# Four more groups of the convolution input product by Strassen's scheme in the projection phase, and half the filler work in the second attention

## The reference

```
h = rms_norm(x, norm1_g)
proj = einsum('bsd,de->bse', h, w_in)          # w_in 1024 x 6144
q, k, v, bg, cg, xc = split(proj)              # six times 1024 features
y_attn = chunked_relpos_attention(q, k, v, ...)  # 16 heads of 64, own chunk of 64 and the 8 before
y_conv = bg * conv_width3(cg * xc)
gates  = sigmoid(einsum(h, w_gate) + b_gate)   # w_gate 1024 x 2048
merged = g_attn * (y_attn @ w_attn_proj) + g_conv * (y_conv @ w_conv_proj)
x = x + merged @ w_out
x = x + square(relu(rms_norm(x, norm2_g) @ w_up)) @ w_down
```

## Time and profile before

| | us |
|---|---|
| median of 3 runs | 2182.41 |
| lowest, highest | 2175.3, 2184.18 |
| the profiled execution's own time | 2176.62 |
| its span, first to last instruction | 2174.9 |

### The profile page before, as it was taken

The page is one execution under the profiler, slowest core; times in us unless marked ns, Lnnn a source line. Parts: engine busy times, 40 slices in busy tenths (PEclk is TensorE's granted clock), DMA queues, the critical chain, the costliest instruction groups (busy, mean ns, idle before and its releaser), DMA issues.

```text
span 2174.9 us, 29102 instructions
## 1 busy us (share of the span) xinstructions
PE 2147.4 (99%) x10450; PEld 1788.1 (82%) x10450; DVE 1480.9 (68%) x2585; ACT 950.3 (44%) x1696; POOL 999.6 (46%) x701
## 2 busy tenths in 40 slices
PE   8999999999999999999999999999999999999999
PEld 8888888888777888888888888788878888788887
DVE  7776775255875666666666658642786777898886
ACT  5555425343232555555555531211555455533332
POOL 3232465454545331313132246547465655666564
PEclk9999999999999999999999999999999999999999
DMA  6320123332135332324243256315144445826433
GB/s 230 104 76 21 45 94 148 126 117 101 55 116 156 103 94 88 99 77 112 67 109 82 75 185 248 115 49 184 59 132 157 167 150 180 328 93 227 151 121 116
DMA packets 198606, 269.34 MB, mean 124 GB/s; under 512 B 58136, under 2 KB 116280, under 8 KB 198368
## 3 DMA queue, kind: packets, MB, share of 16 engines
q1 hardware_dynamic: 124880, 201.38, 27.1%
q10 hardware_dynamic: 73616, 66.49, 10.0%
HBM read 191.23 MB, written 85.00 MB: 127 GB/s over the span
## 4 chain that ended last, share of the span: by engine, by line
PE 82%; DVE 8%; ACT 3%; issue 3%; POOL 2%; DMA 1%; ACTq 1%; POOLq 0%; DVEq 0%; SPq 0%
PE ps L204 71%; PE ps L2333 3%; PE ps L2308 2%; PE ps L2320 2%; PE ps L776 1%; PE ps L751 1%; PE ps L762 1%; DVE k_lo L2553 1%; POOL w_lo L3191 1%; DVE a_lo L446 1%; POOL w_lo L1887 1%; DVE qkv_head_stat L2145 1%; PE ps L2345 1%; DVE pt_lo L2601 0%; ACT pt_hi L2487 0%
## 5 line engine op out<-in xcount | busy, mean ns | idle before, releaser
L204 PE MATMUL ps<-a_hi,w_hi 128*128 128x512 f32 x1376 | 537.1, 407 | 6.0 <-POOL w_lo L1887 3.7
L159 POOL TENSOR_TENSOR w_hi<-w_raw,zero 128x512 fp32r<-128x512 f32 x172 | 201.2, 1200 | 735.9 <-PE ps L204 612.4
L204 PE MATMUL ps<-a_hi,w_lo 128*128 128x512 f32 x1376 | 516.9, 393 | 0.0
L204 PE MATMUL ps<-a_lo,w_hi 128*128 128x512 f32 x1376 | 514.0, 391 | 0.0
L204 PE MATMUL ps<-w_hi,a_hi 128*128 128x512 f32 (+1 forms) x960 | 369.4, 385 | 7.3 <-POOL w_lo L1887 3.5
L204 PE MATMUL ps<-w_hi,a_lo 128*128 128x512 f32 (+1 forms) x960 | 367.6, 383 | 0.0
L204 PE MATMUL ps<-w_lo,a_hi 128*128 128x512 f32 (+1 forms) x960 | 367.5, 383 | 0.0
L204 PEld LDWEIGHTS ps<-a_hi,w_lo 128*128 128x128 f32 x1376 | 258.4, 188 | 57.6
L204 PEld LDWEIGHTS ps<-a_hi,w_hi 128*128 128x128 f32 x1376 | 258.9, 188 | 50.0 <-POOL w_lo L1887 4.5
L204 PEld LDWEIGHTS ps<-a_lo,w_hi 128*128 128x128 f32 x1376 | 259.8, 189 | 40.8
L164 POOL TENSOR_TENSOR w_lo<-w_raw,w_hi 128x512 fp32r<-128x512 f32 x172 | 243.9, 1449 | 3.4
(11 more groups left out here) (307 smaller groups left out, 3938.1 us busy)
## 6 DMA issues: line engine op xcount, KB each, us to landing
mlp_part<-u_parts SPq DMA_DIRECT2D x26, 1024.0 KB, 7.9
w_raw<-in_w_in_dram SPq DMA_DIRECT2D x24, 1024.0 KB, 5.3
feat_fm<-stage ACTq DMA_DIRECT2D x68, 256.0 KB, 2.1
u_parts<-mlp_acc SPq DMA_DIRECT2D x28, 512.0 KB, 2.8
u_parts<-res SPq DMA_DIRECT2D x28, 512.0 KB, 2.8
conv_in<-feat_fm ACTq DMA_DIRECT2D x24, 512.0 KB, 5.1
res<-in_x_dram SPq DMA_DIRECT2D x16, 512.0 KB, 6.5
w_raw<-in_w_out_dram SPq DMA_DIRECT2D x8, 1024.0 KB, 5.0
```

What stands on the lines that cost most here:

```text
L159: hi = nc.gpsimd.tensor_tensor(w_hi[slot][:, k:k + 2, :], w_raw[:, k:k + 2, :], zero[:, 0:1].unsqueeze(2).to_broadcast([P, 2, CW]), ALU.add)
L204: last = nc.tensor.matmul(out_of(o), lhs, rhs(o), start=first and n == 0, stop=final and n == 2)
```

## The change

1. `BCX_GROUPS` goes from 1 to 5: `phase_qkv` makes five groups of 512 columns by seven products each. Two sets of raw weight tiles take turns (`chunk_sides`), two sets of accumulator quarters too (`home`), and PSUM goes round four pairs of banks (`pair`). SP loads a group's weights two groups ahead.
2. In `phase_qkv` two of the four normalisations of each unit come one position later (`normed_in`), behind the next unit's or group's weight sum.
3. `phase_attention` gets 9 chunks of filler in place of 17 (`FILL_CHUNKS`): one ahead, one for each pair, spread evenly over all 130 steps (`filled_to`). `phase_merge` begins at gate chunk 7 as before. The loops over pairs are written out.

```diff
-        BCX_GROUPS = 1
+        BCX_GROUPS = 5
+        FILL_CHUNKS = 9
...
+                def pair(s):
+                    return (s - G_LAST) % 4 if s < G_LAST + 4 else (0, 1, 0)[s - G_LAST - 4]
...
+                def chunk_sides(g):
+                    return (as_chunk(rc), as_chunk(rb)) if g % 2 else (w_raw[:, :, :], as_chunk(rd))
...
+                def home(g, r):
+                    return (1, 1 - r) if g % 2 else (0, r)
...
+                def normed_in(s):
+                    n = s - 1 if s % 7 in (4, 5) else s - 2 if s >= 7 and s % 7 in (0, 1) else None
+                    return n
...
                     for g in range(NG):
                         sp.wait_ge(*low_w.at(NS + 7 * (g + 1)))
-                        load_weights(sp, W_BCX2 + 1, W_BCX2 + 2)
+                        if g + 2 < NG:
+                            load_group(g + 2, 0)
+                            load_group(g + 2, 1)
+                        elif g + 2 == NG:
+                            load_first()
+                        else:
+                            load_weights(sp, W_BCX2 + 1, W_BCX2 + 2)
...
-                        if s and (s - 1) % 7 in DONE:
-                            norm_heads(s - 1)
+                        if normed_in(s) is not None:
+                            norm_heads(normed_in(s))
...
                         if i == 0:
                             weight_sum(position(s, "m6"))
-                            norm_heads(NS - 1)
+                            if s == NS:
+                                norm_heads(NS - 2)
                             weight_sum(position(s, "m5"))
+                            if s == NS:
+                                norm_heads(NS - 1)
...
-            TAIL = 2 * (STEPS + 2)
+            FILLED = 4 * (fill_chunks - 1)
+            PARTS = 2 * (STEPS * pairs + 2)
+            def filled_to(part):
+                return FILLED * KB * part // PARTS
...
-                feed(block, w_start, 2 * pairs + 1, lambda j: (mm_h, j * 4 + 4))
+                feed(block, w_start, fill_chunks, lambda j: (mm_h, j * 4 + 4))
...
-                    body(0, True, False)
-                    with eng.Fori(0, pairs - 2) as j:
-                        body(j + 1, False, False)
-                    body(pairs - 1, False, True)
+                    for i in range(pairs):
+                        body(i, i == 0, i == pairs - 1)
...
+                        part = 2 * (STEPS * i + n) + h
+                        begin, end = filled_to(part), filled_to(part + 1)
...
-                            elif n % 2 == 0:
-                                product_out(i, n // 2 - 1)
-                            else:
-                                product_store(i, n // 2 - 1)
+                            step = STEPS * i + n
+                            if step in STORE_AT:
+                                product_store(STORE_AT[step])
+                            if step in OUT_AT:
+                                product_out(OUT_AT[step])
...
-            opened, banks_read = phase_merge(W_GATE + 5 + 2 * BCX_GROUPS, feat_stored, banks_read)
+            opened, banks_read = phase_merge(W_BCX2 + FILL_CHUNKS, feat_stored, banks_read)
```

More of the change, by code:

```diff
@@ L1928, in _ @@
                     for s in range(NS, NP):
-                        p, i = ORDER[s % 7], s % 7
+                        p, before = ORDER[s % 7], user_before(s, pair)
                         pe.wait_ge(*low_w.at(s + 1))
[L1931 to L1939, removed]
+                        if before is None:
+                            pe.wait_ge(*added.at(added_to(NS - 2 + pair(s) // 2, 1 + 2 * (pair(s) % 2))))
+                        else:
+                            if before % 7 in COPIED:
+                                pe.wait_ge(*b_copied.at(b_copied_to(before)))
+                            if before % 7 in ADDED:
+                                pe.wait_ge(*b_added.at(b_added_to(before)))
                         high, low = operand(p)
@@ L1990, in first_high @@
                         for k in (0, 4):
[L1991 removed]
+                            last = nc.scalar.activation(w_hi[slot_of(W_BCX2)][:, k:k + 4, :], first_raw[:, k:k + 4, :], ACT.Copy)
                         last.then_inc(hi_done, 1)
@@ L2032, in _ @@
                             copy_tile(s, 0)
-                        if squared_now:
-                            root(s - 1)
+                        if ready is not None:
+                            root(ready)
                         if i in COPIED:
@@ L2203, in phase_qkv, with phase_attention @@
                     [store_q[0, 1].at(32), store_q[1, 1].at(32), b_store[0].at(16 * NG), b_store[1].at(16 * NG)])
-        def phase_attention(pairs, src, q_col, k_col, v_col, back, ext, norm_gains, w_start, dst, banks_read, ready_first, ready_rest):
+        def phase_attention(pairs, src, q_col, k_col, v_col, back, ext, norm_gains, w_start, fill_chunks, dst, banks_read, ready_first, ready_rest):
             nslot = back + 2
@@ L2368, in product, with product_part @@
                             last.then_inc(mm_h, 1)
-                    def product_part(i, n, h, last):
-                        part = 2 * n + h
-                        ends = (8 * KB * part // TAIL, 8 * KB * (part + 1) // TAIL) if last else (2 * part, 2 * part + 2)
-                        for x in range(ends[0] // KB, (ends[1] - 1) // KB + 1):
-                            ks = range(max(ends[0] - x * KB, 0), min(ends[1] - x * KB, KB))
-                            product(i * 2 + (w_start + 1 + x // 4), x, ks, i * 8 + (EARLY + x))
+                    def product_part(i, n, h):
+                        part = 2 * (STEPS * i + n) + h
+                        begin, end = filled_to(part), filled_to(part + 1)
+                        for x in range(begin // KB, (end + KB - 1) // KB):
+                            ks = range(max(begin - x * KB, 0), min(end - x * KB, KB))
+                            product(w_start + 1 + x // 4, x, ks, EARLY + x)
                     for x in range(EARLY):
@@ L2628, in body @@
                             link.close(PER)
-                    pair_loop(dve, body)
-            products = 8 * pairs + EARLY
-            return ([(st_h[s], 16 * (4 * pairs + EARLY // 2 + 1)) for s in range(2)],
+                    pair_loop(body)
+            products = FILLED + EARLY
+            return ([(st_h[s], 16 * (products // 2 + 1)) for s in range(2)],
                     [[(o_done, 8 * pairs + 1), (ev_h, products - 1)], [(ev_h, products), (lo_r, 4 * pairs + 1)],
```

167 lines of the change are left out of this document (92 added, 75 removed).

## The result

The changed kernel takes **2278.36 us** (median of 4 runs, 2276.57 to 2279.49) against 2180.64 for the kernel before, timed beside it (4 runs, 2175.3 to 2184.18): ratio **1.0449**, 95% interval 1.0427 to 1.0471. It is slower, as forecast: 2274 had been said, and 2252 to 2305. The profiled execution has a span of 2275.8 us, 100.9 above the 2174.9 of before.

The account below looks back on a forecast made before the run. PE was taken to bound the kernel, in the attention with a ring of DVE and ACT just beneath. 2176.6 + 152.3 - 48 - 10 = 2271, plus half of 5.8 for the median: 2274 us, range 2252 to 2305.

Parts of the forecast that it names:

- Part 1: phase_qkv: four more groups at 38.1 us each, all on the path, +152.3 us.
- Part 3: phase_qkv: normalisations behind the weight sums remove three stops for weights and the slow clock behind two, -10 us.
- what is late next: phase_qkv: once the stops are gone, `root` on ACT, behind the group's first copy, could be late; no separate size.
- Part 2: phase_attention: eight chunks less of filler, a pair of heads 6.35 us shorter, -48 us in all (bounds -64 and -24).
- the ring of DVE and ACT: phase_attention: maximum, exponential, pt_hi, pt_lo never overlap, 3.34 us a step; about 63.8 us a pair, PE's 69.8 above.
- the pair of 63.5: phase_attention: forecast time for two heads after the change, 63.8 - 2.0 + 1.7 = 63.5 us.
- The term for the copies that fall away: phase_attention: ACT makes 4 of 8 filler copies a pair fewer, 0.49 us each, 2.0 us a pair off the ring.
- 1.75 of 2.4 in the last pair: Attention before the change: a last-pair head loses 2.4 us of PE's filler, yet only 1.75 came through.
- Part 4: SP's loads, written-out loops, POOL's splitting and phase_merge, costed at nothing, between -3 and +5 us for all.
- Rival B: Thinned attention: granted clock falls; 2534 us at 1.2 GHz throughout, 2342 for half of PE's work; chance 7%.
- wrong if the clock were under 0.95: Sign for the attention: a clock under 0.95 in the profile after would show the mechanism wrong.
- Rival C: phase_qkv: groups don't run clean, m6's sum late at four new changes, +21 us; 2302, or 2307 as median; chance 10%.

Follow-up runs that it names:

- e9: Kernel of e5 with the filler shared out as before the change (64 blocks in each of the first seven pairs): 2172.0 us, ratio 0.9971.
- e5: Changed kernel with one group, 17 chunks of filler and the normalisations back ahead of the weight sums: 2169.83 us, ratio 0.9958.
- e6: Changed kernel with the high by high matmul of every filler block run twice: 2278.18 us, ratio 1.0458.
- e7: Changed kernel with only the high by high matmul left in each filler block: 2290.42 us, ratio 1.0516.
- e4: Changed kernel with ACT's copy of the turned probabilities (pt_hi) ahead of the next tile's exponential: 2255.03 us, ratio 1.0382.
- e10: Changed kernel with ACT's copy of a filler product in the attention cut to 8 of 512 columns: 2269.71 us, ratio 1.0411.
- e2: Changed kernel with two groups and 15 chunks of filler: 2182.44 us, ratio 1.0022 against the kernel before.

## Why the prediction was right, and where it wasn't

- **Part 1, the groups: right.** 38.4 us each, +153.5 for +152.3.
- **Part 3, the order of the normalisations: right in size.** The attention starts 141.1 later; less the 153.5, and with 1.7 us that e9, which has neither part, also starts earlier (703.57 against 705.30), -10.7 is left for the -10; by e5, which starts at 705.02, it would be -12.1. No stop and no slow stretch is left in `phase_qkv`, and e5 shows that the order makes them. Of "what is late next" the wrong thing was named; it shows only with one group. The rows also left out the fourth stop, of 0.81 us.
- **Part 2, the attention: right in kind, too large in size**, -40.1 for -48, and of the 40.1 some 4 are the loops' (14 heads at 0.30 in e9), so 36. That the ring of DVE and ACT bounds it is shown from three sides: more of PE's work costs next to nothing (e6), less of it gives nothing (e7), another order on ACT alone gives 23 us (e4). What failed is the pair of 63.5, which was 64.9. Where the clock is 1.00 and up to the eighth head, the pair is 2 x 31.33 = 62.7, and 63.3 with the loops' 2 x 0.30 put back, close to the 63.5. Two things came on top. The clock had been put at 1.00; its fall costs 0.5 us a head, 1.0 a pair. And all pairs had been taken alike, but from the ninth head on the mean is 33.09 against 31.83. The term for the copies that fall away, 2.0 us a pair, each whole in the ring, isn't borne out either: e10 gives 0.4 a pair at a like clock in the first half, and more in the second.
- **"The ring's own length is 63.8, and PE lies 6 above it"** was too plain. With a margin of 6.1 us, the first cut of 5.4 would have come through whole; 1.5 did (e2). So the waits put down to PE in the earlier trace rows aren't a slack that can be taken off one for one. That steps with large and small blocks share it out unevenly is my reading, not shown by a run. I had the sign of this in hand, 1.75 of 2.4 in the last pair, and priced it too low.
- **Part 4, at nothing: wrong by about 4 us.** The written-out loops were priced from -3, since their register instructions run while the engine waits. e9 shows that they bring 4.1 us in the attention where PE is full. Which engine's loop cost it wasn't tried.
- **Rival B, the clock: alive, and small.** I had let it decide at single gaps near 2.85 us. PE's waits in the same 400 us after (the third number is the longest):

```profile
PE ps L2362 <- DVE st L2631: 31.3, 25, 2.2
PE ps L2387 <- DVE pt_lo L2650: 31.0, 33, 1.9
PE ps L2374 <- DVE pt_lo L2650: 12.0, 22, 1.4
```

  None is above 2.2 us, and the clock was at 0.94 all the same. By the sign "wrong if the clock were under 0.95" the mechanism would be wrong; e4, e6 and e7 say that it holds, so the sign was a bad one. It costs 6 to 8 us, not the 68 of half of PE's work at 1.2 GHz. PE isn't the bound, and as I read it only the value matmuls and turnings in the ring pay.
- **Rival C's price** adds the whole 5.8 us to its 2302, where the forecast adds half to its 2271. Alike, it would be 2305; nothing else hangs on it.

So the total came within 4.4 us in part by luck, because errors met. Against the 2271 of the sum the profiled execution took 2277.6. The cut of the filler gave 12 us less than said (36 for 48) and the groups cost 1.2 more; against that stand 4 us from the loops, put at nothing, 1.7 that arise ahead of the attention in e9 too, and 0.7 from part 3. The half of 5.8 added at the end took up 2.9 of the 6.7 that remained.

After the change a head grows from 31.3 us at the start to 33.8 near the end. It does so at a clock of 1.00 (e6: 31.6, then 32.5 in the second half) and with small copies (e10: 31.7, then 32.4), and doesn't with the order of e4 (30.84, then 30.82). The growth sets in with the ninth head, and there the program changes: 256 blocks of filler are spread over 260 half-steps, so the copies of finished products (`OUT_AT`) stand in an odd step up to step 65 and in an even one from step 70, in the ninth head. Of the two copies a head, one is followed up to there by a wait for PE's turning, so the ring loses nothing by it, and the other at full clock by `pt_hi` at once, so it lies in the ring whole. From step 70 on both are followed by `pt_hi` at once. The first kind, and the second:

```profile
912.71 0.57 ACT L2490 ACTIVATE stage<-ps 128x512 f32<-128x512 f32 x1
913.47 0.28 ACT L2541 ACTIVATE pt_hi<-ps 128x128 fp32r<-128x128 f32 x1 [0.19 <-PE ps L2374]
```
```profile
1191.13 0.60 ACT L2490 ACTIVATE stage<-ps 128x512 f32<-128x512 f32 x1
1191.62 0.76 ACT L2541 ACTIVATE pt_hi<-ps 128x512 fp32r<-128x512 f32 x2
```

One copy more in the ring is 0.49 us a head, of the 0.8 by which e6's heads grow at a like clock (31.60 to 32.4). No run moved the copies alone, so an experiment for it is lacking. Open is the rest of the growth, and why the two longest heads, 33.76 and 33.81, are longer still.

## What to carry to other kernels

An engine that is busy 99% may have a ring of two others just beneath it: look in the table of waits for two engines that wait for each other for most of their idle time, and ask for each stage how much of a cut would come through before moving work out of it. Work that fills such a stage is nearly free there and costs full price anywhere else, even when its new form is an eighth cheaper. If the stage must be shorter, change the order on one engine of the ring first (23 us here, for two lines moved), and keep PE full, as a thinned stage also pays in its clock. And look at which steps the small instructions fall on when work is spread anew: in one step the engine had to wait anyway, in the next it had not.

## What was not expected of the hardware

- The granted clock was 0.94 over 400 us with PE busy 81% (325 of 400) and no gap over 2.2 us; 1.00 at 88% (351 of 400, e6), 0.85 at 66% (264 of 400, e7). In `phase_qkv` before, the falls stood behind single stops of 2.85 and 3.54 us; the stop of 1.10 had none. Here it falls without any stop of that length.
- Taking PE's matmuls away made the kernel slower (e7: 12 us), at a clock of 0.85. Where the clock is at its lower level, value matmuls stand 0.21 us apart and not 0.12 (shown after the change).
- Loops over pairs of heads, written out, brought about 4 us (e9, 0.30 a head) though their register instructions seemed covered.
